# The four modulation tiles of the feed-forward stage, multiplied on VectorE instead of TensorE

## The reference

```python
cond = jax.nn.silu(c.astype(F32))
for i in range(DEPTH):
    mod = cond @ mod_w[i].astype(F32) + mod_b[i].astype(F32)     # 1024 x 6144 weights per layer
    sh1, sc1, g1, sh2, sc2, g2 = jnp.split(mod[:, None, :], 6, axis=-1)
    y = (rms_norm(h, norm1_g[i]).astype(F32) * (1.0 + sc1) + sh1)
    # layer 0: conformer convolution;  layer 1: S5 state-space layer
    h = h + g1 * y
    y = (rms_norm(h, norm2_g[i]).astype(F32) * (1.0 + sc2) + sh2)
    # layer 0: swiglu(y) = (silu(y @ w_gate) * (y @ w_up)) @ w_down, hidden width 2816
    # layer 1: the same in 8 experts of width 3584, the best 2 for each token
    h = h + g2 * y
return rms_norm(h, final_norm_g)
```

## Time and profile before

| | |
|---|---|
| median of three runs | 1583.22 us |
| the profiled execution: device time | 1582.53 us |
| its span in the trace | 1580.7 us |
| TensorE busy | 1502.2 us (95%) |
| VectorE busy | 1286.5 us (81%) |
| ScalarE busy | 1023.5 us (65%) |
| GpSimd busy | 217.4 us (14%) |
| feed-forward stage in the trace | 188.5 to 393.4 us |

### The profile page before, as it was taken

How to read it: one execution, slowest core, us unless ns; L and a number is a source line. 1 busy time by engine, 2 the same in 40 slices (tenths; PEclk the granted TensorE clock), 3 DMA queues, 4 the chain that set the end, 5 groups by cost and what they waited for, 6 DMA issues and landing times.

```text
span 1580.7 us, 23513 instructions
## 1 busy us (share of the span) xinstructions
PE 1502.2 (95%) x8591; PEld 1263.7 (80%) x8591; DVE 1286.5 (81%) x1426; ACT 1023.5 (65%) x1045; POOL 217.4 (14%) x251
## 2 busy tenths in 40 slices
PE   6997899999799889999999999999999999999996
PEld 4775899999568768888888888888888888877885
DVE  4796467555885589889889989889888999999995
ACT  4556545554224467777777777777776888878773
POOL 0771136532590000000000000000000000000000
PEclk9998999999799989999999999999999999999998
DMA  9955376665475769999999999999937999999991
GB/s 310 325 192 191 107 248 230 231 234 206 157 258 172 267 230 349 374 340 361 366 343 360 368 342 364 362 344 363 361 139 273 355 357 382 363 323 382 383 371 41
DMA packets 231210, 463.32 MB, mean 293 GB/s; under 512 B 18255, under 2 KB 57687, under 8 KB 231127
## 3 DMA queue, kind: packets, MB, share of 16 engines
q1 hardware_dynamic: 229591, 461.55, 81.7%
q10 hardware_dynamic: 1536, 0.68, 0.2%
HBM read 461.15 MB, written 1.05 MB: 292 GB/s over the span
## 4 chain that ended last, share of the span: by engine, by line
PE 81%; DVE 7%; POOL 5%; ACT 3%; issue 1%; DMA 1%; SPq 0%; ACTq 0%; DVEq 0%; POOLq 0%
PE bank L2204 12%; PE bank L2207 12%; PE bank L2210 12%; PE bank L1864 12%; PE bank L2344 5%; PE bank L2347 4%; PE bank L2019 3%; PE bank L2300 2%; PE bank L2301 2%; PE bank L2313 2%; PE bank L2308 2%; PE bank L2312 2%; DVE bank L1337 2%; PE bank L1852 1%; PE bank L1948 1%
## 5 line engine op out<-in xcount | busy, mean ns | idle before, releaser
L1619 DVE TENSOR_TENSOR wlo<-ring,whi 128x2048 fp32r<-128x2048 f32 x210 | 477.1, 2289 | 68.5 <-PE bank L2210 55.5
L1029 ACT ACTIVATE whi<-ring 128x2048 fp32r<-128x2048 f32 x210 | 400.9, 1918 | 117.8 <-PE bank L2207 117.7
L1125 ACT ACTIVATE whi<-ring 128x2048 fp32r<-128x2048 f32 x126 | 237.8, 1914 | 44.1 <-PE bank L2308 32.7
L2204 PE MATMUL bank<-whi,xe_hi 128*128 128x512 f32 x560 | 219.6, 392 | 7.2 <-ACT whi L1029 7.2
L2207 PE MATMUL bank<-whi,xe_lo 128*128 128x512 f32 x560 | 218.9, 391 | 0.0
L1735 DVE TENSOR_TENSOR wlo<-ring,whi 128x2048 fp32r<-128x2048 f32 x84 | 190.8, 2281 | 7.1 <-ACT whi L1125 6.9
L1255 DVE TENSOR_TENSOR ring_lo<-ring,ehi 128x2048 fp32r<-128x2048 f32 x45 | 106.3, 2362 | 58.3 <-ACT ehi L795 58.3
L2210 PE MATMUL bank<-wlo,xe_hi 128*128 128x512 f32 x560 | 150.5, 391 | 0.0
L2204 PEld LDWEIGHTS bank<-whi,xe_hi 128*128 128x128 f32 x560 | 105.8, 189 | 29.4 <-issue 7.4
L2210 PEld LDWEIGHTS bank<-wlo,xe_hi 128*128 128x128 f32 x560 | 105.7, 189 | 22.1
L2207 PEld LDWEIGHTS bank<-whi,xe_lo 128*128 128x128 f32 x560 | 105.7, 189 | 22.0
(11 more groups left out here) (459 smaller groups left out, 2874.9 us busy)
## 6 DMA issues: line engine op xcount, KB each, us to landing
ring<-in_moe_w_gate_dram SPq DMA_DIRECT2D x112, 1024.0 KB, 7.0
ring<-in_moe_w_up_dram SPq DMA_DIRECT2D x112, 1024.0 KB, 7.0
ring<-in_moe_w_down_dram SPq DMA_DIRECT2D x112, 1024.0 KB, 6.9
ring<-in_mod_w_dram SPq DMA_DIRECT2D x24, 2048.0 KB, 9.7
ring<-in_ffn_w_gate_dram SPq DMA_DIRECT2D x11, 1024.0 KB, 6.2
ring<-in_ffn_w_up_dram SPq DMA_DIRECT2D x11, 1024.0 KB, 8.6
ring<-in_ffn_w_down_dram SPq DMA_DIRECT2D x11, 1024.0 KB, 5.0
ring<-in_conv_w_pw_dram SPq DMA_DIRECT2D x8, 1024.0 KB, 12.3
```

The source lines that it names most:

```text
L1029: act.activation(whi[:, n % HI_SLOTS, :], ring[:, s * HW:(s + 1) * HW], ACT.Copy).then_inc(hi_ready, 1)
L1125: act.activation(whi[:, q % HI_SLOTS, :], ring[:, s * HW:(s + 1) * HW], ACT.Copy).then_inc(hi_ready, 1)
L1619: v.tensor_tensor(wlo[:, n % LO_SLOTS, :], ring[:, s * HW:(s + 1) * HW], whi[:, n % HI_SLOTS, :].bitcast(F32), ALU.subtract).then_inc(lo_r ...
L2204: mm(o[:, :], xh, hi[:, w:w + 512], start=first, stop=False)
```

## The change

VectorE multiplies tiles 12 to 15. For each tile there are eight steps, one for each 128 rows of the weights: a `tensor_scalar` and seven `scalar_tensor_tensor` of 128x512 elements. They multiply the weights by the conditioning value of each partition and add onto bank 6; the last one writes `tmp`. Four steps stand behind the gated product of half 2b, and four behind that of half 2b+1, each ahead of `split_lo`. All but the last are linked. TensorE's `mod_partial` and ScalarE's `mod_copy` of these tiles go. `mod_sums` takes a column of ones in place of the column of 1/32, and moves one block later, behind the down product of block b; `mod_vector` moves with it. The slot of the tile is now released by VectorE's eighth step.

```diff
+        def by_vector(m):
+            return 2 * FFN_MODS <= m < 2 * S5_MODS
+
+        def copies_after(m):
+
+            return m - sum(by_vector(k) for k in range(m))
...
 # ScalarE, feed-forward loop
-                if b in FFN_MOD_BLOCKS:
-                    m = 2 * FFN_MODS + FFN_MOD_BLOCKS.index(b)
-                    mod_copy(m)
...
-                if b in FFN_MOD_BLOCKS and m % 2:
-                    mod_vector(m // 2)
+                if b - 1 in FFN_MOD_BLOCKS[1::2]:
+                    mod_vector(FFN_MODS + FFN_MOD_BLOCKS.index(b - 1) // 2)
...
 # VectorE
+            def mod_products(m, kcs):
+
+                n = WHERE[("mod", m)]
+                w, acc_, dst = early(n, KC), psum[6][:, :], mod_place(m)[2]
+                for kc in kcs:
+                    cc = cond_late[:, kc, 0:1]
+                    if kc == 0:
+                        v.wait_ge(cond_ready, 2)
+                        v.wait_ge(mod_acc, 2 * FFN_MODS)
+                        v.wait_ge(arr[slot_of(n)], arrived_count(n))
+                        link(v.tensor_scalar(acc_, w[:, kc, :], cc, None, ALU.mult))
+                    elif kc < KC - 1:
+                        link(v.scalar_tensor_tensor(acc_, w[:, kc, :], cc, acc_, ALU.mult, ALU.add))
+                    else:
+                        v.wait_ge(mod_sum, m)
+                        v.scalar_tensor_tensor(dst, w[:, kc, :].rearrange("p (a n) -> p a n", a=2), cc,
+                                               acc_.rearrange("p (a n) -> p a n", a=2), ALU.mult, ALU.add).then_inc(mod_part, 1)
...
                     v.tensor_tensor(hid[:, f % 4, :], psum[4 + f % 2][:, T:2 * T], tmp[:, f % 2, 0:T],
                                     ALU.mult).then_inc(hid_ready, 1)
+                    if b in FFN_MOD_BLOCKS:
+                        mod_products(2 * FFN_MODS + FFN_MOD_BLOCKS.index(b), range(4 * (f % 2), 4 * (f % 2) + 4))
                     split_lo(UNIT[("gu", b, f % 2)] + 2)
...
 # TensorE
-                    pe.wait_ge(mod_acc, m - 1 if 2 <= m < 2 * FFN_MODS else m)
+                    pe.wait_ge(mod_acc, m - 1 if 2 <= m < 2 * FFN_MODS else copies_after(m))
...
-                pe.wait_ge(mod_acc, m + 1)
+                if by_vector(m):
+                    pe.wait_ge(mod_part, m + 1)
+                else:
+                    pe.wait_ge(mod_acc, copies_after(m + 1))
                 for o in range(4):
                     ins = mm(bank[:, 4 * h + o:4 * h + o + 1], part[:, o // 2, (o % 2) * P:(o % 2) * P + P],
-                             sum_col[:, :], start=True, stop=True)
+                             ones[:, 0:1] if by_vector(m) else sum_col[:, :], start=True, stop=True)
...
-                if b in FFN_MOD_BLOCKS:
-                    m = 2 * FFN_MODS + FFN_MOD_BLOCKS.index(b)
-                    pe.wait_ge(cond_ready, 2)
-                    pe.wait_ge(var_ready, 3)
-                    mod_partial(m)
                 if b:
                     down(b - 1)
-                if b in FFN_MOD_BLOCKS:
-                    mod_sums(m)
+                if b - 1 in FFN_MOD_BLOCKS:
+                    pe.wait_ge(var_ready, 3)
+                    mod_sums(2 * FFN_MODS + FFN_MOD_BLOCKS.index(b - 1))
```

## The result

| | before | after |
|---|---|---|
| median of 10 runs each, on one chip | 1583.97 us (1582.99 to 1586.65) | 1588.47 us (1587.62 to 1590.80) |
| ratio, 95% interval | | 1.0029 (1.0021 to 1.0037) |
| profiled execution, its span | 1582.53, 1580.7 | 1589.98, 1588.2 |

The change makes the kernel 0.29% slower, 4.5 us. I forecast 1585.4, 0.14% slower, with 55% on a change within 0.2%. The direction was right and the time lies inside the range of 1581.5 to 1589.0, but the size was too small: 1588.47 is outside the forecast's own 1583.5 to 1587.0, and the change is above 0.2%.

A forecast was written before the change was run, and what follows sets the result against it. TensorE was taken to set the time, with VectorE's chain deciding where it waits. Block 2 +3.4, block 4 0, blocks 6 and 8 -0.6 each: +2.2 us on 1583.22, so 1585.4 us; range 1581.5 to 1589.0.

The forecast's parts named there:

- rival in which the steps pay more, or take turns with GpSimd: VectorE's steps each cost 0.1 us more, 3.2 in all: +5.4, 1588.6 us; chance 18%.
- Blocks 6 and 8: Blocks without GpSimd in the way: VectorE's chain takes 24.00 us instead of 25.49; net 0.61 us won in each.
- rival in which TensorE goes on bounding: Feed-forward stage: TensorE bounds, VectorE's work fits in its idle time; -8.1 us, 1575.1; chance 6%.
- Block 2: Block with four tables and GpSimd's turns: group ends 2.53 us later, with 0.88 for the sums 3.4 us lost.
- rival in which the turns with GpSimd cost little: Block 2 loses 0.5 us, block 4 wins 0.9, the others 1.2: -1.6, 1581.6 us; chance 17%.
- two groups 11.61: TensorE's pair of groups behind the column sums takes 11.61 us, 0.09 more than two times 5.76.
- the remaining 40 matmuls, 5.06: TensorE's matmuls left behind a block's last `split_lo` take 5.06 us.
- about 1.0, 1.7 and 2.4 us: TensorE's waits in block 2, given in the rival where its clock falls there.
- rival to which I gave 12%: TensorE's clock falls in block 2, costing 2.7 us on top of the sum: +4.9, 1588.1 us; chance 12%.
- a granted clock below 1 in the stage: Sign in the new trace's feed-forward stage that would show the prediction wrong: TensorE's granted clock falling below 1.
- Block 4: GpSimd's turns start in block 3: won 1.49 + 0.3, lost 0.9 + 0.88 us, so nothing (-0.9 to +0.5).
- a shift passes through: Behind the feed-forward stage: what follows starts from its end on TensorE, so a shift there passes on.

The follow-up runs named there:

- before, high part early: Kernel before the change, ScalarE making the high part ahead of its tables, VectorE splitting behind three tables at the latest: 1585.18 us, ratio 1.0001.
- before, last product early: Kernel before the change, product of the last S5 modulation tile made one group earlier: 1584.05 us, ratio 0.9999.
- before, all three: Kernel before the change, ScalarE's high part ahead of its tables, S5 weights prepared earlier, tables spread 2, 3, 3 instead of 0, 4, 4: 1587.91 us, ratio 1.0016.
- after, again: The changed kernel run once more without any edit: 1590.14 us, ratio 1.0035 to the kernel before.
- after, high part early: Changed kernel, ScalarE making the high part ahead of its tables, VectorE splitting behind three tables at the latest: 1586.64 us, ratio 1.0004.
- after, weights early: Changed kernel, GpSimd's two preparations of S5 weights moved from tables 6 and 12 to 2 and 3: 1590.52 us, ratio 1.0033.
- after, last product early: Changed kernel, product of the last S5 modulation tile made one group earlier: 1587.08 us, ratio 1.0013.
- after, blocks 3, 5, 7, 9: Changed kernel with its four tiles in blocks 3, 5, 7 and 9 instead of 2, 4, 6 and 8: 1584.08 us, ratio 0.9996.
- after, all three: Changed kernel, ScalarE's high part ahead of its tables, S5 weights prepared earlier, tables spread 2, 3, 3 instead of 0, 4, 4: 1580.70 us, ratio 0.9976.
- after, all three, last product early: "after, all three" plus the product of the last S5 modulation tile made one group earlier: 1581.17 us, ratio 0.9974.
- after, all three, three and five: "after, all three" with each tile's eight steps divided three and five instead of four and four: 1583.24 us, ratio 0.9982.

## Why the prediction was right and wrong

**The steps.** Forecast 0.75 us each, 0.785 apart; measured 0.744 to 0.754, 0.78 to 0.79 apart. The nearest row, a `scalar_tensor_tensor` that reads a bank at 746 ns, was the right one to take. The 691 ns for a `tensor_tensor` that the prediction quotes from the Trainium skill, "VectorE: DVE Perf Modes", section on the TRN2 errata, would have been short of it by 0.06 us. The rival in which the steps pay more, or take turns with GpSimd, is out.

**Blocks 6 and 8.** Forecast 24.00 us from `hid` to the end of group (b+1,1); measured 332.03 - 307.93 = 24.10, and 23.97 two blocks on. The wait ahead of the down product is 0.58 (forecast 0.5); that in the group is 0.42 of idle time and makes the matmuls start 0.6 late (0.65). The gains of the two blocks, with the later sums, are 0.52 and 0.64 (0.61 each). The rival in which TensorE goes on bounding is out: VectorE was busy 11.07 of 20.19 us, and these waits came nonetheless.

**Block 2.** Forecast 2.53 us later, and the sums. Measured: group (3,1) ends at 257.98, which is 6.15 after 251.83, or 3.60 without the 2.55 that lay ahead of the stage. The order of turns came as worked out. VectorE and then GpSimd in order of time in block 2 of after, which answer to the earlier trace rows:

```profile
229.31 0.74 DVE L1395 TENSOR_SCALAR bank<-ring,cond_late 128x512 f32<-128x512 f32 x1
230.09 2.34 DVE L1397 SCALAR_TENSOR_TENSOR bank<-ring,cond_late,bank 128x512 f32<-128x512 f32 x3
232.47 2.66 DVE L1259 TENSOR_TENSOR ring_lo<-ring,ehi 128x2048 fp32r<-128x2048 f32 x1
235.05 2.63 DVE L1415 TENSOR_TENSOR hid_lo<-hid,hid_hi 128x256 fp32r<-128x256 f32 x1
```

```profile
229.19 1.91 POOL L699 TENSOR_TENSOR caT<-cT,sp 128x1024 f32<-128x1024 f32 x1
231.06 1.91 POOL L700 TENSOR_TENSOR cts<-cT,sp 128x1024 f32<-128x1024 f32 x1
233.05 4.34 POOL L703 TENSOR_TENSOR caT<-caT,cts 128x1024 f32<-128x1024 f32 x1
```

The steps run beside GpSimd's first two instructions, neither of them slower. The split waits 0.4 us for the second to end, GpSimd's third starts and is held until the split ends at 235.13, and `hid_lo` ends with it at 237.6. The turns themselves are 0.4 us cheaper than forecast. So the rival in which the turns with GpSimd cost little is out for block 2, too: I gave it 17%.

**The step that failed** is "two groups 11.61", "the remaining 40 matmuls, 5.06", taken for block 2 as for the others. I had put the three waits there at "about 1.0, 1.7 and 2.4 us". They came as 1.0, 1.1 and, for the third, 0.76 and 1.11 a little apart. TensorE in order of time in blocks 2 and 3 of after:

```profile
235.18 0.39 PE L2046 MATMUL bank<-hid_hi,ehi 128*128 128x256 f32 x1 [1.01 <-DVE ring_lo L1259]
...
243.30 1.22 PE L1888 MATMUL bank<-y_hi,ring_lo 128*128 128x256 f32 x8 [1.14 <-DVE ring_lo L1259]
...
249.11 1.22 PE L1888 MATMUL bank<-y_hi,ehi 128*128 128x256 f32 x8 [0.76 <-ACT ehi L802]
251.44 2.08 PE L1888 MATMUL bank<-y_hi,ring_lo 128*128 128x256 f32 x8 [1.11 <-DVE ring_lo L1259]
```

The eight at 251.44 already take 2.08 us instead of 1.22: the clock has fallen. In the stretches it is read directly (third column from the end):

```profile
248.00:252.00 4.00, 2.13 (x13) 1.72 (x13) 2.73 (x3) 3.97 (x7) 3.33 (x7) 0.93 1.06 381
252.00:256.00 4.00, 4.00 (x25) 4.00 (x24) 2.62 (x2) 0.17 (x1) 2.58 (x1) 0.65 0.57 200
```

It was granted 0.65 on the mean over four microseconds in which TensorE was busy throughout, so part of them at the lower of its two levels, 1.2 GHz. The 40 matmuls took 6.54 us, 1.48 more. That is the rival to which I gave 12%, at a little over half its price of 2.7. The prediction had named a granted clock below 1 in the stage as a sign that it is wrong, and by that sign it is. The Trainium skill, "TensorE: Matmul & The Clock Gate", Part 1, has idleness as what brings the throttled state back; block 2's trace agrees with that, but I had read it as one long gap, and here no single wait was longer than 1.14 us. That this rival's 1588.1 is so near the measured time is luck: its fall gave 1.5 us, and the rest came from the S5 stage, at which no rival looked.

**Block 4.** Forecast nothing (down to -0.9); measured 0.69 won. The turns cost 0.3 us, not 0.9, since GpSimd's third instruction was nearly through: `ring_lo` took 2.57 us and `hid_lo` 0.41. So the stage's sum is 3.6 + 0.88 - 0.69 - 0.52 - 0.64 = +2.6, and it came near the forecast +2.2 because block 2 lost 1.5 to the clock, and block 4 and the turns gave 1.1 back.

**What follows the stage.** I wrote that "a shift passes through". That is the second step that failed. TensorE in order of time at the end of the S5 stage, before and then after:

```profile
450.39 3.50 PE L1948 MATMUL bank<-ring,cond_late 128*32 128x512 f32 x16
...
469.15 0.63 PE L2090 MATMUL bank<-prod,cT 128*32 128x128 f32 x8 [0.75 <-POOL prod L749]
...
471.13 1.92 PE L1948 MATMUL bank<-ring,cond_late 128*32 128x512 f32 x16
474.72 0.63 PE L2090 MATMUL bank<-prod,cT 128*32 128x128 f32 x8 [1.67 <-POOL prod L749]
```

```profile
453.08 1.92 PE L1972 MATMUL bank<-ring,cond_late 128*32 128x512 f32 x16
...
474.20 1.07 PE L2113 MATMUL bank<-prod,cT 128*32 128x128 f32 x8 [3.03 <-POOL prod L756]
...
476.06 1.87 PE L1987 MATMUL bank<-sum_col,modacc_s 128*128 128x1 f32 x8
477.85 3.64 PE L1972 MATMUL bank<-ring,cond_late 128*32 128x512 f32 x16
```

GpSimd's products set the pace of this stage in both: 474.20 is 469.15 plus 5.05, of which 5.17 is the shift so far. Before, the clock fell in the middle of the stage (the product at 450.39 took 3.50), where TensorE is ahead of GpSimd, and near the end all ran at full clock. After, it stayed full in the middle, TensorE was further ahead, waited 3.03 us instead of 0.75 for the same `prod`, and the clock fell in that wait, with a product of 16 still to do before GpSimd's last `prod` can be used. The stretches of after:

```profile
470.56:474.56 4.00, 0.97 (x16) 0.67 (x14) 3.97 (x3) 0.00 (x0) 3.75 (x4) 0.84 1.06 343
474.56:478.56 4.00, 4.00 (x28) 2.95 (x28) 0.67 (x1) 0.00 (x0) 3.92 (x3) 0.50 0.63 199
```

I split the S5 stage at the end of GpSimd's last `prod`, in all kernels with eight steps or none:

```
                               to GpSimd's last prod   from there to z_hi   last product
before                                81.27                 5.59               1.92
before, high part early               81.37                 5.59               1.92
before, last product early            81.15                 5.60               1.92
before, all three                     81.59                 7.29               3.47
after                                 80.36                 8.97               3.64
after, again                          80.37                 8.96               3.64
after, high part early                81.39                 5.61               1.92
after, weights early                  81.58                 7.16               3.35
after, last product early             80.41                 7.13               1.92
after, blocks 3, 5, 7, 9              80.82                 6.15               3.31
after, all three                      80.52                 6.23               3.42
after, all three, last product early  80.58                 7.43               1.92
after, all three, three and five      81.38                 8.94               3.64
```

The first part moves by about 1 us, the second by 3.4, and the second follows the clock: 5.6 where nothing falls, 6.2 where only the last product is slow, 7.1 to 7.4 or 9.0 where more is. With the last product moved, the changed kernel's tail drops by 1.84 us and that of before by nothing. So the 2.5 us are 3.4 of slow clock at the tail less 0.9 that GpSimd was earlier. The slow clock also reaches past the last `z_hi`, and the 0.74 us of the fourth row of the result go with it: 82.8 us in the three kernels with a tail of 9.0 (after, again, and three and five), 81.8 to 82.3 in all others but the two with the early high part. When the fall comes stays open: in a wait of 3.03 us or some 2 us behind the same wait, and "before, all three", "weights early" and "blocks 3, 5, 7, 9" had one in the middle and one at the end. It repeated in the changed kernel; it wasn't tried whether it can be steered.

## What to carry to other kernels

When work is moved to an engine with idle time, follow that engine in order of time from the input of the moved work to the next thing it owes: here VectorE was idle for 45% of a block, and still the kernel with the change came out 4.5 us slower than before, or, with three edits that shorten that chain, 4.5 us faster. Several waits of 1 us, one behind another, must be priced as a possible fall of TensorE's clock; in this stage, moving the work a block on was enough to undo it. And a stage that another engine paces doesn't pass a shift through unchanged, so its end belongs to the sum.

## What the runs showed of the hardware

The clock falls without a long gap. In the changed kernel's stage it fell behind waits of 1.14, 0.76 and 1.11 us within ten microseconds; elsewhere, in the changed kernel and in others, in or behind single waits of 2.67, 3.03, 3.27 and 4.61, at the latest some 2 us behind them, and in the S5 stage of before 2 us behind one of 1.26. It stayed full behind 1.67 (before), 1.24 (after, at 463.9) and behind 0.58 and the 0.42 that follows in block 6. It even fell with no wait over 0.15 us in the ten microseconds ahead of it: in the kernel with blocks 3, 5, 7 and 9 at some 441.4 us, at the end of a row of small matmuls in the S5 stage, with TensorE busy throughout (clock in the third column from the end):

```profile
435.00:439.00 4.00, 4.00 (x50) 3.23 (x46) 3.90 (x11) 2.57 (x4) 3.75 (x4) 1.00 0.78 258
439.00:443.00 4.00, 4.00 (x48) 2.62 (x50) 2.98 (x8) 0.00 (x0) 3.78 (x4) 0.81 0.93 351
```

So a wait is not the only thing that brings a fall; what else does wasn't tried.

A fall cost 1.5 us on 40 matmuls, 1.6 on the 48 of a down product, 1.7 on a product of 16 with 512 columns.

Steps that read one SBUF tile and a bank, with the scalars of the partitions in SBUF, ran in 0.74 to 0.75 us beside GpSimd's instructions and did not slow them (1.91), while the split, which reads two SBUF tiles, took turns with them. The Trainium skill, "SBUF — State Buffer", section "Who interferes with whom", names the number of SBUF inputs as what decides; the trace agrees, and shows that the scalar for each partition does not count as one.
